# Gate sums spread over the partitions: one plain fp32 product, or two rounded parts with two rounded products

## The reference, cut to what matters

```python
m_lat = (silu_c @ ada_w[i] + ada_b[i]).reshape(B, N_MOD, 1, D)      # 6 parts of 1024
m_ctx = (silu_cc @ ada_w[i] + ada_b[i]).reshape(N_MOD, D)
h_lat = modulate(rms_norm(x_lat, norm_g[i, 0]), m_lat[:, 0], m_lat[:, 1])
...                                                                  # the mixer gives y_lat
x_lat = x_lat + m_lat[:, 2] * rms_norm(y_lat, norm_g[i, 1])          # part 2: the first gate
h = modulate(rms_norm(x_lat, norm_g[i, 2]), m_lat[:, 3], m_lat[:, 4])
x_lat = x_lat + m_lat[:, 5] * rms_norm(sqrelu_mlp(h, mlp_w1[i], mlp_w2[i]), norm_g[i, 3])   # part 5: the second gate
```

## Time and profile before

| | |
|---|---|
| median of 3 runs | 2007.76 us (2007.71 to 2008.89) |
| the profiled execution | 2008.43 us, span 2006.6 us |
| TensorE busy | 1961.1 us, 98% |
| VectorE busy | 1357.7 us, 68% |
| ScalarE busy | 885.6 us, 44% |
| GpSimd busy | 254.4 us, 13% |

### The profile page before, as it was taken

The page is one execution under the profiler, slowest core; times in us unless marked ns, Lnnn a source line. Parts: engine busy times, 40 slices in busy tenths (PEclk is TensorE's granted clock), DMA queues, the critical chain, the costliest instruction groups (busy, mean ns, idle before and its releaser), DMA issues.

```text
span 2006.6 us, 27568 instructions
## 1 busy us (share of the span) xinstructions
PE 1961.1 (98%) x10390; PEld 1638.3 (82%) x10390; DVE 1357.7 (68%) x2172; ACT 885.6 (44%) x1513; POOL 254.4 (13%) x333
## 2 busy tenths in 40 slices
PE   8999999999999999999999999999999999989998
PEld 4877788888888777888999888878888878878897
DVE  5888768777756644488987675666755467567655
ACT  3433354333333443575554224534233354556554
POOL 2101011111110200411101001111110021331000
PEclk9999999999999999999999999999999999999999
DMA  8434235655553451268864422645555245236753
GB/s 305 135 102 126 84 96 182 203 177 171 183 186 99 149 162 39 86 228 270 269 218 156 148 96 65 198 158 178 152 173 154 81 148 168 92 99 221 230 181 114
DMA packets 191859, 315.20 MB, mean 157 GB/s; under 512 B 14653, under 2 KB 114328, under 8 KB 191728
## 3 DMA queue, kind: packets, MB, share of 16 engines
q1 hardware_dynamic: 162512, 210.09, 32.5%
q0 software_dynamic: 29216, 103.36, 17.2%
HBM read 312.35 MB, written 1.05 MB: 156 GB/s over the span
## 4 chain that ended last, share of the span: by engine, by line
PE 90%; DVE 4%; issue 2%; ACT 2%; POOL 1%; DMA 0%; SPq 0%; POOLq 0%; DVEq 0%; ACTq 0%
PE bank L680 26%; PE bank L687 24%; PE bank L686 24%; PE bank L690 11%; PE bank L685 2%; PE bank L683 2%; PE bank L750 1%; ACT junk L1567 1%; POOL st L3157 1%; DVE wl L2166 1%; DMA raw<-in_ada_w 0%; DVE X L2288 0%; PE bank L1056 0%; DVE acc L2191 0%; POOL wl L3085 0%
## 5 line engine op out<-in xcount | busy, mean ns | idle before, releaser
L1551 ACT ACTIVATE wh<-raw 128x1024 fp32r<-128x1024 f32 (+4 forms) x390 | 399.3, 1030 | 602.7 <-PE bank L687 571.3
L2166 DVE TENSOR_TENSOR wl<-raw,wh 128x1024 fp32r<-128x1024 f32 (+3 forms) x372 | 440.2, 1189 | 296.3 <-ACT wh L1551 295.4
L680 PE MATMUL bank<-HH,wh 128*128 128x256 f32 (+1 forms) x1552 | 517.6, 333 | 2.4 <-DVE HH L2271 1.4
L687 PE MATMUL bank<-HH,wl 128*128 128x512 f32 (+1 forms) x1232 | 415.1, 337 | 0.0
L686 PE MATMUL bank<-HL,wh 128*128 128x512 f32 (+1 forms) x1232 | 415.0, 337 | 0.0
L2191 DVE SCALAR_TENSOR_TENSOR acc<-ada,sc,acc 128x512 f32<-128x512 f32 x518 | 362.2, 745 | 2.3
L680 PEld LDWEIGHTS bank<-HH,wh 128*128 128x128 f32 x1552 | 294.5, 190 | 31.4 <-issue 5.7
L680 PE MATMUL bank<-wh,UH 128*128 128x512 f32 x768 | 303.0, 395 | 0.0
L687 PE MATMUL bank<-wh,UL 128*128 128x512 f32 x768 | 301.6, 393 | 0.0
L686 PE MATMUL bank<-wl,UH 128*128 128x512 f32 x768 | 300.8, 392 | 0.0
L686 PEld LDWEIGHTS bank<-HL,wh 128*128 128x128 f32 x1232 | 231.7, 188 | 27.9 <-issue 2.2
(11 more groups left out here) (342 smaller groups left out, 2592.7 us busy)
## 6 DMA issues: line engine op xcount, KB each, us to landing
raw<-in_mlp_w SPq DMA_DIRECT2D x256, 512.0 KB, 4.2
ada<-in_mod_w POOLq DMA_DIRECT2D x96, 512.0 KB, 4.7
ada<-in_ada_w POOLq DMA_DIRECT2D x80, 512.0 KB, 4.7
raw<-in_ml_w_qkvo SPq DMA_DIRECT2D x28, 512.0 KB, 4.1
raw<-in_conv_w_in SPq DMA_DIRECT2D x24, 512.0 KB, 3.5
raw<-in_ada_w SPq DMA_DIRECT2D x12, 512.0 KB, 6.0
raw<-in_mla_w_o SPq DMA_DIRECT2D x8, 512.0 KB, 4.2
raw<-in_gla_w_v SPq DMA_DIRECT2D x8, 512.0 KB, 3.7
```

Source lines behind the costliest of these rows:

```text
L680: pe.matmul(o, sh, mh, start=start, stop=False, skip_group_check=True)
L687: return pe.matmul(o, sl, mh, start=False, stop=stop, skip_group_check=True)
L1551: act.activation(k.wh[n % NSPL][:, 0:m], k.raw[(NDIRECT + n) % NRAW][:, 0:m], ACT.Copy).then_inc(*k.w_hi.up("w hi", n))
L2166: dve.tensor_tensor(k.wl[n % NSPL][:, 0:m], k.raw[(NDIRECT + n) % NRAW][:, 0:m], k.wh[n % NSPL][:, 0:m].bitcast(F32), ALU.subtract).then_i ...
```

## The change

The sum of a gate chunk is cut in two rounded parts. ScalarE copies `acc` to the rounded type (`Gh`, which lies where `G` lies), VectorE subtracts that from `acc` (`accl`, which lies where `acc` lies), and TensorE makes two rounded products with rounded ones and adds them in the same bank. Both parts are entries of the closing list: the copy with the count 1, the subtraction with the count 2, and the product stays at 3. The copy waits for the chunk's sum and for the last readers of the gate rows that it overwrites; the subtraction waits for the copy; the products wait for both. The tile of ones is made by VectorE from the identity at the start in place of GpSimd's load.

```diff
@@ Walk.step
         elif end is not None:
+            if end[0] == "finish" and end[2] in (2, 5):
+                self.closing.append([1, key, ("leading",) + end[1:5] + (False,)])
+                self.closing.append([2, key, ("low",) + end[1:5] + (False,)])
             self.closing.append([self.lag, key, end])
@@ Kern.lay_out
-        self.G = sb("G", [128, 2, D])
+        with ExitStack() as s1:
+            self.G = sb("G", [128, 2, D], F32, s1)
+        self.Gh = sb("Gh", [128, 2, D], F32R)
...
+        self.accl = sb("accl", [128, 2, 2, 512], F32R)
...
+        self.ones = sb("ones", [128, 128], F32R)
@@ pe_program, close
-                    mm(b[:, :], k.ones[:], k.acc[:, n % 2, ty, :]).then_inc(*b.filled())
+                    w.wait_ge(*at("sum hi", n, ty))
+                    mm(b[:, :], k.ones[:], k.Gh[:, ty, ch * 512:ch * 512 + 512], True, False)
+                    w.wait_ge(*at("sum lo", n, ty))
+                    mm(b[:, :], k.ones[:], k.accl[:, n % 2, ty, :], False, True).then_inc(*b.filled())
@@ act_program
+    gate_before = {}
     def close(c):
-        pass
+        if c[0] == "leading":
+            li, part, ch, types = c[1:5]
+            n = CHUNK[li, part, ch]
+            w.wait_ge(*at("ada sum", n, 3))
+            for ty in types:
+                if (ch, ty) in gate_before:
+                    for t in range(2):
+                        w.wait_ge(*at("gated", *gate_before[ch, ty], ch, ty * 2 + t))
+                else:
+                    for half in range(2 if ch == 0 else 1):
+                        w.wait_ge(*ps.of("dcol", ch, half).full())
+                gate_before[ch, ty] = li, part
+                act.activation(k.Gh[:, ty, ch * 512:ch * 512 + 512], k.acc[:, n % 2, ty, :],
+                               ACT.Copy).then_inc(*k.sum_hi.up("sum hi", n, ty))
@@ dve_program, close
+        if c[0] == "low":
+            n, ch, types = CHUNK[c[1:4]], c[3], c[4]
+            for ty in types:
+                o = k.acc[:, n % 2, ty, :]
+                w.wait_ge(*at("ada sum", n, 3))
+                w.wait_ge(*at("sum hi", n, ty))
+                dve.tensor_tensor(k.accl[:, n % 2, ty, :], o, k.Gh[:, ty, ch * 512:ch * 512 + 512].bitcast(F32),
+                                  ALU.subtract).then_inc(*k.sum_lo.up("sum lo", n, ty))
@@ dve_program, start
+    w.wait_ge(*at("ident"))
+    dve.tensor_scalar(k.ones[:], k.ident[:], 0.0, 1.0, ALU.mult, ALU.add).then_inc(*own.up("ones"))
@@ pool_program, start
-    pool.dma_start(k.ones[:], k.cap("ones")).then_inc(*k.ones_in.up("ones", by=16))
```

More of the change, by code:

```diff
@@ L466, in __init__ @@
         self.blocks = list(weight_stream(A))
-        self.ident_in, self.ones_in, self.c_in = sig("ident_in"), sig("ones_in"), sig("c_in")
+        self.ident_in, self.c_in = sig("ident_in"), sig("c_in")
         self.x_in = [sig(f"x_in{t}") for t in range(4)]
@@ L483, in __init__ @@
         self.ada_sum, self.bias_cols, self.mod_done, self.gate_rows = sig("ada_sum"), sig("bias_cols"), sig("mod_done"), sig("gate_rows")
+        self.sum_hi, self.sum_lo = sig("sum_hi"), sig("sum_lo")
         self.mean_in, self.rstd_in = sig("mean_in"), sig("rstd_in")
@@ L519, in lay_out @@
         self.ada = [sb(f"ada{i}", [128, 2, 512]) for i in range(NADA)]
-        self.acc = sb("acc", [128, 2, 2, 512])
+        with ExitStack() as s1:
+            self.acc = sb("acc", [128, 2, 2, 512], F32, s1)
+        self.accl = sb("accl", [128, 2, 2, 512], F32R)
         self.gb = sb("gb", [128, 2, 512])
         self.drow = [[self.G[0:2, ch, part * 512:part * 512 + 512] for part in range(2)] for ch in range(2)]
-        self.ident, self.ones = sb("ident", [128, 128]), sb("ones", [128, 128])
+        self.ident = sb("ident", [128, 128])
+        self.ones = sb("ones", [128, 128], F32R)
         self.ta = Ring([sb(f"ta{i}", [128, 512]) for i in range(2)], at)
@@ L732, in close @@
                     for m in range(4):
-                        p = mm(b[:, i * 4 + m:i * 4 + m + 1], k.acc[:, n % 2, ty, m * 128:m * 128 + 128], k.ones[:, 0:1])
+                        p = mm(b[:, i * 4 + m:i * 4 + m + 1], k.acc[:, n % 2, ty, m * 128:m * 128 + 128], k.ones[:, 0:1].bitcast(F32))
                 p.then_inc(*b.filled())
@@ L1863, in log_gates @@
                 g = k.gx[:, r, t, :]
-                act.activation(g, g, ACT.Ln, bias=k.ones[:, 0:1]).then_inc(*k.log_act.up("log act", r, t))
+                act.activation(g, g, ACT.Ln, bias=k.ones[:, 0:1].bitcast(F32)).then_inc(*k.log_act.up("log act", r, t))
         def q_out(n):
@@ L2006, in gates @@
             w.wait_ge(*at("ones"))
-            act.activation(k.mfa[:], k.mfa[:], ACT.Ln, bias=k.ones[:, 0:1]).then_inc(*own.up("forget log"))
+            act.activation(k.mfa[:], k.mfa[:], ACT.Ln, bias=k.ones[:, 0:1].bitcast(F32)).then_inc(*own.up("forget log"))
         def rows(r):
@@ L2220, in close @@
     def close(c):
-        if c[0] == "columns":
+        if c[0] == "low":
[6 more added lines that the diff above has]
+                                  ALU.subtract).then_inc(*k.sum_lo.up("sum lo", n, ty))
+        elif c[0] == "columns":
             b = ps.of("cols", c[1])
```

## The result

The change made the kernel slower, by little more than the 0.2% that can be told apart. In 14 runs of each on the same chips the median is 2014.35 us (2009.46 to 2017.91) against 2009.58 us (2007.71 to 2010.80); the ratio is 1.0023, with a 95% interval of 1.0015 to 1.0032. The profiled execution took 2013.62 us with a span of 2011.8, 5.2 us more than before. The forecast was 2006.3 us, 1.5 us less than before, and its range ended at 2010.5.

A forecast was written before the change was run, and what follows sets the result against it. TensorE's in-order stream, busy 98% of the span, was taken as the bound; 9.8 us gained less 0.82, 0.40, 3.2, 1.5 and 2.4 leaves 1.5, so 2006.3 us; own range 2003.8 to 2009.5, rivals left out above 2010.5.

The forecast's parts named there:

- the size of the gain: At the 24 gate products on TensorE, two rounded products for 0.863 us cost 0.454: 0.409 each, 9.8 us in all.
- five late places: Gates at 236, 338, 851, 1699 and 1796 us: parts come late, losing 0.82, 0.40, 3.2, 1.5 and 2.4 us.
- The other 11 chunks (17 products) have a tick or more between.: At the remaining gate chunks both parts were to be ready in time, with no wait of TensorE.
- The reading that the forecast used at 338 us: Second gate of layer 0: subtractions follow VectorE's additions ending at 337.97; stream back at 339.48, 0.40 us lost.
- So is one that TensorE has to wait inside it: TensorE's stream of weight blocks: each microsecond of waiting in it costs a microsecond of the run.
- (a): Rival: parts in time nearly everywhere or waits taken back; 1998.0 us without waits, 2002.1 with half back; chance 0.17.
- The mixer behind 1701 us: Range end: the 1.1 us lost at 1699 can vanish in the mixer, where TensorE is idle 9.5 of 90 us.
- (b): Rival: ScalarE, held by the sums, delays weight copies; 0.85 us at all 16 chunks, 12.1 slower, 2019.9; chance 0.08.
- (c): Rival: a rounded product with ones as weights still costs 0.43 us; 8.3 us slower at most, 2016.1; chance 0.03.
- One end of the range: Lower end, given as 2003.8 us: the mixer hides 1.1 us and the start gives 0.7.

The follow-up runs named there:

- a3_both: Changed kernel with the low part one tick earlier and the new entries also counted and made in quiet stretches: 1998.74 us, 0.9954 of the kernel before.
- a4_fill: Changed kernel with 13, 10 and 10 rounded products that nobody reads put into the three long waits: 2009.06 us, 1.0004 of the kernel before.
- b3_work: Changed kernel's copies and subtractions all made, but the old plain fp32 product, with TensorE waiting for neither part: 2008.42 us, 1.0000 of the kernel before.
- the first four kernels: Variants of the changed kernel: low part earlier, quiet stretches used, both, long waits filled; the kernel before had a median of 2008.56 us beside them.
- b1_one_place: Changed kernel with the low part one tick earlier only at the second gate of layer 1, second half: 2008.80 us, 1.0002 of the kernel before.
- a2_quiet: Changed kernel with leading and low entries also counted and made in quiet stretches, the product left in place: 2005.18 us, 0.9981 of the kernel before.
- b2_waits: Changed kernel's copies, subtractions and TensorE waits for both parts, but the old plain fp32 product: 2025.55 us, 1.0073 of the kernel before.

## Why the prediction was wrong

**Right: the size of the gain.** 0.409 a product and 9.8 us in all; a3_both measured 9.8, though its interval of 6.8 to 11.9 us can't tell 9.8 from 10.4; the steps of 0.227 and 0.863 us can. The Trainium skill's rule ("FP8 and Floating Point Precision", section "TensorE Precision Notes") would have said 10.4, an estimate. The four passes stand in that section; the single pass of the reduced product is read from the contrast there.

**Right: five late places and their sizes.** Forecast 0.82, 0.40, 3.2, 1.5 and 2.4 us of delay; the starts of the gate products in the changed kernel's trace give 0.84, 0.37, 3.2, 1.5 and 2.35, and the products behind them start some 0.1 us later still. At 850 us the leading part came at 849.62 and the low one at 850.98, where the stream would have had them at 847.51 and 0.23 after the first: 3.2 us. VectorE's order there is the one that was read from the earlier trace rows, with the new subtraction behind the four of the weights:

```profile
845.70 4.62 DVE L2197 TENSOR_TENSOR wl<-raw,wh 128x1024 fp32r<-128x1024 f32 x4
850.24 0.69 DVE L2258 TENSOR_TENSOR accl<-acc,Gh 128x512 fp32r<-128x512 f32 x1
```

**Wrong: "The other 11 chunks (17 products) have a tick or more between."** It failed at one of the 11, the second gate of layer 1, second half. There is a tick between, but VectorE makes four additions of the next layer in it. It also came late to them: the weight subtraction ahead of them waited 1.92 us for a copy of ScalarE that had itself waited 1.22 us for its load.

```profile
944.72 1.06 ACT L1566 ACTIVATE wh<-raw 128x1024 fp32r<-128x1024 f32 x1 [1.22 <-DMA raw<-in_mlp_w]
...
945.88 1.23 DVE L2197 TENSOR_TENSOR wl<-raw,wh 128x1024 fp32r<-128x1024 f32 x1 [1.92 <-ACT wh L1566]
947.03 2.74 DVE L2222 SCALAR_TENSOR_TENSOR acc<-ada,sc,acc 128x512 f32<-128x512 f32 x4
949.68 0.69 DVE L2258 TENSOR_TENSOR accl<-acc,Gh 128x512 fp32r<-128x512 f32 x1
```

950.42 less 947.51 and a step of 0.23 is 2.7 us. The additions could be read in the trace of before, where the product is issued in the middle of them:

```profile
946.75 2.73 DVE L2191 SCALAR_TENSOR_TENSOR acc<-ada,sc,acc 128x512 f32<-128x512 f32 x4
...
947.60 1.02 PE L690 MATMUL bank<-acc,ones 128*128 128x512 f32 x2
```

VectorE's next work starts at 949.40. The reading that the forecast used at 338 us puts the subtraction there, 949.40 to 950.09, and the low part was needed at 947.83: an estimate of 2.3 us late, from the trace of before alone. The count of ticks was taken for the distance in time. How much of the 2.7 us the late load has was not tried.

**Wrong: the term that the sum did not have.** "So is one that TensorE has to wait inside it" priced a wait at its length. A wait of 2.2 to 2.8 us was followed by 3.4 us at half clock, 1.6 us more, three times: 4.8 us by the rows, 4.3 by a4_fill. Either missing term alone turns the sign: 1.5 us less becomes 1.2 more with the place at 950 us, and 3.3 more with the clock. The trace of before has the pattern in its own transitions, behind the wait of 2.89 us at 869 us among others; the clock's column of the busy time by stretch shows it:

```profile
871.40:874.80 3.40, 3.23 (x14) 3.10 (x15) 3.25 (x7) 2.56 (x7) 2.28 (x4) 0.50 0.73 225
```

**The sum again**, against the profiled execution: -1.5 forecast, +2.7 for the place at 950 us (counted from where the forecast had the stream), +4.8 for the clock: +6.0. Measured +5.2. The rest is where else the two executions were at half clock: the one before for 3.4 us at 670 us and for 6.8 at 1813, the changed one not at the former (-1.6) and for 10.2 at 1817 (+0.8; the changed kernel was 5.1 us behind at 1804 us and 6.0 at 1825). With these it is +5.2. That part is not laid to the change.

**Rivals.** (a) did not come: the waits arose at all five places, and nothing took them back. The mixer behind 1701 us did not either, although the range had its 1.1 us as an end. (b) did not come: ScalarE was held by a sum for 4.3 us in all, and b3_work shows that it cost nothing. (c) was wrong by every step of 0.23. The slower side came by a late place and a loss of clock that none of the three named. One end of the range was added wrongly: 2006.3 less 1.1 and 0.7 is 2004.5, not 2003.8; the result lies at the other side, so nothing hangs on it.

**Open.** The changed kernel's runs are spread over 8.5 us, those of before over 3.1 (4.4 in the 27 runs beside the first four kernels) and of a3_both over 1.8 in 5 runs. But a4_fill, whose three waits are filled, is spread over 8.8 us, so the spread is not explained by those waits alone. The mean clock of the changed kernel's runs goes with the time, from 0.994 at 2009.46 us to 0.989 at 2017.91, so different numbers of stretches at half clock seem to be behind it. What decides whether a wait brings one is not shown: 2.19 us did in the changed kernel's trace and did not in b1_one_place's.

## What to carry to other kernels

A wait put into a saturated stream of products costs its length and can cost the clock of what follows; here three waits of 2.2 to 2.8 us cost some 1.6 us each on top in the profiled execution, and products that nobody reads, in the waits, bought some 4 us back. When one late operand becomes two made by other engines, find for each place what stands ahead of the making in that engine's program order, in us and not in ticks, above all where a demand flushes what was put off and where loads are late. Splitting a plain fp32 product of 512 columns into two rounded ones is worth 0.41 us, as long as both parts are old when they are asked for.

## What was not expected of the hardware

Behind three waits of TensorE (2.8 us in two pieces, 2.5 and 2.2 us, at 849, 948 and 1798 us) the granted clock was 0.50 for 3.4 us; behind those of 1.36 and, in a2_quiet, 1.20 us it stayed at 1.00, as it did behind one of 2.19 us in b1_one_place and one of 1.69 us in b2_waits. Plain products of the identity with itself, 8 to 15 of them in a wait, stood beside a granted clock of 1.00 in place of 0.72 in the transition at 860 us and of 0.84 in place of 0.69 in the one at 1803.
